# Mixer phase of a two-block transformer kernel: two heads across the partitions, block-diagonal 128x128 products, attention written between the levels of the triangular inverse

## The reference, cut to what matters

```python
z = rmsnorm(h, mix_norm_g) @ w_in                     # 256 x 3072
y_pool = pool_mixer(z[:, :256])                       # 4 windowed means, 4 small products, a scale
y_rwkv = rwkv7_mixer(z[:, 256:1280])                  # 4 heads of 64
y_diff = diff_attention(z[:, 1280:])                  # 4 heads, two score maps each
h = h + concat([y_pool, y_rwkv, y_diff]) @ w_out
# rwkv7_mixer: token shift, low-rank decay/a/gate, normalized key, the wkv7 recurrence, group norm, gate
# diff_attention: q, k RMS-normalized over 64 channels per (token, head, c);
#   p = softmax(s0 + bias) - lam * softmax(s1 + bias);  o = p @ v;  RMS norm of o over 128, gain
```

## Time and profile before

| | us |
|---|---|
| median of 3 runs | 3002.99 (2996.99 to 3004.98) |
| the profiled execution's own time | 3003.37 |
| its span | 3001.6 |
| mixer phase in it, first transpose to the last addition | 2177.7 to 2595.5 |

### The profile page before, as it was taken

One profiled execution on the slowest core, in us unless ns is written; L12 is line 12 of the kernel. 1 busy time (PEld: TensorE's weight loads), 2 busy tenths in 40 slices (PEclk: granted clock), 3 DMA queues, 4 the chain that ended last, 5 costly groups with the idle time before them and its releaser, 6 DMA issues.

```text
span 3001.6 us, 42198 instructions
## 1 busy us (share of the span) xinstructions
PE 2597.4 (87%) x16904; PEld 2319.8 (77%) x16904; DVE 2282.8 (76%) x3225; ACT 874.9 (29%) x1292; POOL 266.1 (9%) x100
## 2 busy tenths in 40 slices
PE   6979999999999996689999999999875674595898
PEld 6857999999888875379999998888673573474896
DVE  6768897999666777378989996666785645585887
ACT  1000344444555440103444445555312000000000
POOL 0000593000000000005920000000000000000000
PEclk8999999999999997689999999999996555697999
DMA  5624676656777763026765657777551000241554
GB/s 183 179 84 134 203 210 186 191 179 189 244 256 241 243 208 103 32 92 207 210 190 179 191 179 252 255 241 242 181 148 60 1 15 0 81 154 42 148 171 145
DMA packets 201186, 484.00 MB, mean 161 GB/s; under 512 B 23392, under 2 KB 93408, under 8 KB 200480
## 3 DMA queue, kind: packets, MB, share of 16 engines
q1 hardware_dynamic: 194784, 467.75, 50.1%
q10 hardware_dynamic: 6208, 13.56, 1.4%
HBM read 446.62 MB, written 34.60 MB: 160 GB/s over the span
## 4 chain that ended last, share of the span: by engine, by line
PE 58%; DVE 32%; POOL 4%; issue 2%; DMA 2%; ACT 1%; ACTq 0%; DVEq 0%
PE psum L865 23%; PE psum L662 19%; DVE rounded L1251 7%; DVE halves L2021 7%; PE psum L818 6%; DVE halves L2018 5%; POOL rounded L630 4%; PE psum L1040 2%; DVE rounded L1247 2%; DMA sb<-in_u_turned 1%; DVE sb L1764 1%; PE psum L704 1%; PE psum L943 1%; DVE sb L1286 1%; PE psum L941 1%
## 5 line engine op out<-in xcount | busy, mean ns | idle before, releaser
L1251 DVE TENSOR_TENSOR rounded<-sb,rounded 128x1024 fp32r<-128x1024 f32 (+3 forms) x696 | 813.9, 1172 | 243.0 <-ACT rounded L2242 233.4
L662 PE MATMUL psum<-rounded 128*128 128x256 f32 (+1 forms) x4380 | 728.8, 330 | 84.4 <-DVE rounded L1251 42.3
L818 PE MATMUL psum<-rounded 128*128 128x256 f32 x6144 | 774.2, 285 | 12.6 <-POOL rounded L630 12.4
L662 PEld LDWEIGHTS psum<-rounded 128*128 128x128 f32 x4380 | 655.6, 198 | 157.8 <-DVE rounded L1251 38.8
L2242 ACT ACTIVATE rounded<-sb 128x1024 fp32r<-128x1024 f32 x512 | 542.8, 1060 | 788.5 <-PE psum L818 346.6
L818 PEld LDWEIGHTS psum<-rounded 128*128 128x128 f32 x6144 | 748.1, 192 | 15.2 <-POOL rounded L630 15.2
L865 PE MATMUL psum<-rounded,weights 128*128 128x512 f32 x3072 | 697.3, 389 | 0.4 <-ACT sb L2258 0.4
L865 PEld LDWEIGHTS psum<-rounded,weights 128*128 128x128 f32 x3072 | 576.4, 188 | 120.6 <-issue 1.2
L630 POOL TENSOR_TENSOR rounded<-sb,rounded 128x1024 fp32r<-128x1024 f32 x96 | 265.9, 2785 | 1255.8 <-ACT rounded L2242 1255.3
L1247 DVE CAST rounded<-sb 128x1024 fp32r<-128x1024 f32 (+4 forms) x317 | 192.9, 609 | 134.5 <-PE psum L662 110.0
L2021 DVE TENSOR_TENSOR halves<-halves,small 128x1536 bf16<-128x1536 bf16 x128 | 225.0, 1758 | 4.4
(11 more groups left out here) (292 smaller groups left out, 1439.1 us busy)
## 6 DMA issues: line engine op xcount, KB each, us to landing
sb<-in_u_turned SPq DMA_DIRECT2D x256, 512.0 KB, 3.8
sb<-in_peer_v SPq DMA_DIRECT2D x256, 512.0 KB, 3.6
hidden<-sb SPq DMA_DIRECT2D x256, 128.0 KB, 3.8
sb<-hidden SPq DMA_DIRECT2D x256, 128.0 KB, 3.5
sb<-in_ret_w_in SPq DMA_DIRECT2D x48, 512.0 KB, 4.4
sb<-in_ffn_w_up SPq DMA_DIRECT2D x40, 512.0 KB, 4.5
sb<-in_peer_w_q SPq DMA_DIRECT2D x32, 512.0 KB, 4.1
sb<-in_ffn_w_down SPq DMA_DIRECT2D x22, 512.0 KB, 4.0
```

The source lines that it names most:

```text
L662: mm = pe.matmul(o, a[p], b[q], start=(first and i == 0), stop=(last and i == 2), skip_group_check=True)
L818: mm = pe.matmul(ps(bank, 1)[:, 0:T], u[p][:, k * P:(k + 1) * P], hT[:, q, k, :], start=(k == 0 and w == 0), stop=(k == KD - 1 and w == 2))
L1251: vec.tensor_tensor(ring_lo[0:k, part, 0:wide], ring[0:k, slot, 0:wide], ring_hi[0:k, part, 0:wide].bitcast(F32), ALU.subtract).then_inc(c ...
```

## The change

Only the mixer phase and what feeds it are rewritten.

- **Layout.** Two heads lie across the 128 partitions: channel tensors are 128x512 where they were 64x1024, and there are 8 pair units (`PU`) where there were 16 units. Where a product needs both heads apart, one operand is block-diagonal 128x128 (`btB`, `ktB`, `mabA`, `makA`, `makR`, `RB`, `AV`, `Tm`, `TmT`, `Q`, `Mt`), written by quadrants; the zeros are set by GpSimd at the start.
- **Norms.** The sums of squares of q and k are products with a 128x2 matrix (`each`), so 32 numbers a token; one root and one reciprocal on 128x32 (`qki`). k is scaled through a widened copy turned by TensorE (`wide`, "kb"); q's factor goes into the scores' scale. The o norm is a Square with a sum on ScalarE.
- **Weights.** ScalarE makes the high halves of the phase's 56 tiles (`BY_ACT`, `hi_to`), VectorE only the low ones.
- **Parameters** are issued by SP between the tiles of `slots0` from its fourth on, after a wait for the end of the peer phase; the bias by SP after the last tile of `pool_in`, after a wait for `ktB`.
- **Order.** Each engine has a list of named steps and one semaphore; the others wait for a step by name. The preparation lies between the panels; q.k scores, Exp, the pool mixer and the turning of p lie between the levels. Each level is done in two halves of 4 pair units. GpSimd makes `aoff` for levels 1 to 5; the copies of X go to ScalarE. Level 0 needs no product.
- **Softmax.** Four quarters (map, token block): the max as the bias of Exp, the sum from Exp's accumulator, the division folded into the difference.
- **`mix_out`** takes its rows in the order 0, 1, 4, 5, 6, 7, 2, 3 (`MIX_OUT_ROWS`), and begins when the pool part is there; the recurrence's part comes last.

The core of the diff (TensorE, levels and end):

```diff
+                for b in range(1, LEVELS):
+                    pe.wait_ge(*pool_told.of(f"aoff{b}"))
+                    for half, us in zip("AB", HALVES):
+                        pe.wait_ge(*vec_told.of(f"T{b - 1}{half}" if b > 1 else "T0"))
+                        tell(units(6, P, lambda u: a["aoff"][b % 2][:, u, :], of("Tm"), us), f"X{b}{half}")
+                    if b == 1:
+                        tell(turned(0, of("ktB")), "kT")
...
+                    if b == 2:
+                        pe.wait_ge(*act_told.of("aT"))
+                        scores(0)
...
+                    for half, us in zip("AB", HALVES):
+                        pe.wait_ge(*act_told.of(f"X{b}{half}"))
+                        if b < LEVELS - 1:
+                            tell(units(4, P, of("TmT"), of("X"), us), f"T{b}{half}")
+                        tell(units(2, P, of("X"), of("TmT"), us), f"W{b}{half}")
...
+                for half, us in zip("AB", HALVES):
+                    pe.wait_ge(*vec_told.of(f"T5{half}"))
+                    tell(units(4, P + C, of("TmT"), of("AV"), us), f"AV{half}")
+                turn_p(0)
...
+                tell(units(4, 2 * P, of("G1"), of("RB"), [u for u in range(PU) if u % NC_]), "QM")
+                tell(turn_p(1), "pT")
...
+                panel("mix_out", lambda k: hk(MIX_OUT_ROWS[k]), "tokens", 0, D, between=join)
```

VectorE between the levels, ScalarE's high halves and GpSimd:

```diff
+                    if b > 1:
+                        biased(b - 2)
+                    for half, us in zip("AB", HALVES):
+                        part = slice(us[0], us[-1] + 1)
+                        if b < LEVELS - 1:
+                            vec.wait_ge(*pe_told.of(f"T{b}{half}"))
+                            vec.tensor_tensor(a["Tm"][:, part, :], a["Tm"][:, part, :], banks_of(4, us), ALU.add)
+                        vec.wait_ge(*pe_told.of(f"W{b}{half}"))
+                        vec.tensor_tensor(a["TmT"][:, part, :], a["TmT"][:, part, :], banks_of(2, us), ALU.add)
+                    if b > 1:
+                        tops(b - 2)
+                    if b == 4:
+                        combine(0)
...
+            def hi_to(end_):
+                while ahead.n < end_:
+                    n = ahead.n
+                    k, wide = chunk_size[n]
+                    act.wait_ge(ring_loaded[n % RING], 16 * (n // RING + 1))
+                    act.wait_ge(chunks_done, n - SPLIT + 1)
+                    act.activation(ring_hi[0:k, n % SPLIT, 0:wide], ring[0:k, n % RING, 0:wide], ACT.Copy)
+                    ahead.up()
...
+                for b in range(1, LEVELS):
+                    if b > 2:
+                        gp.wait_ge(*pe_told.of(f"X{b - 2}B"))
+                    gp.tensor_tensor(a["aoff"][b % 2], a["mabA"], bcast(a["levels"][:, b, :], 1, PU), ALU.mult)
...
+            def mixer_params(count):
+                if len(mixers_left) == len(params["mixers"]):
+                    sync.wait_ge(phase_done, phases.index("mixers"))
+                for dst, src in mixers_left[:count]:
+                    sync.dma_start(dst, src).then_inc(params_loaded, 16)
```

More of the change, by code:

```diff
@@ L502, in build, with over @@
[L502 to L506 removed]
+                def over(at, *dims):
+                    return Memory(at, 0, at.shape[1]).take(*dims)
+                B2 = (PU, P)
+                hn = m.take(2048)
@@ L1035, in pe_mixers, with tell @@
-                pe.wait_ge(*masked)
-                wait_all(turned)
-                def units(b0, lhs, rhs, first=True, last=True, us=range(UN)):
-                    for u in us:
-                        mm = pe.matmul(ps(b0 + u // 8, 1, C)[:, (u % 8) * C:(u % 8 + 1) * C], lhs(u), rhs(u),
-                                       start=(first and u % 8 == 0), stop=last, skip_group_check=True)
+                told = Count()
+                def tell(mm, name):
+                    pe_told.check(name, told.up())
+                    mm.then_inc(mix_pe, 1)
@@ new lines, in units @@
+                def units(b0, wide, lhs, rhs, us=range(PU), begin_=True, last=True, parts_=P):
+                    per, begun = BANK // wide, set()
+                    for u in us:
+                        b = b0 + u // per
+                        mm = pe.matmul(ps(b, 1, parts_)[:, (u % per) * wide:(u % per + 1) * wide], lhs(u), rhs(u),
+                                       start=(begin_ and b not in begun), stop=last, skip_group_check=True)
+                        begun.add(b)
+                    return mm
@@ L1667, in vec_mixers @@
+                vec.memset(z[:, :, 0:1], 0.0).then_inc(*own.next())
+                split_to(end["slots0"] + 2)
                 vec.wait_ge(params_loaded, loads["mixers"])
                 done()
[L1669 to L1672 removed]
@@ new lines, in vec_mixers @@
+                split_to(end["slots1"] + 3)
+                vec.wait_ge(*act_told.of("z1"))
+                mixed(6, 8, "zm_act")
+                more(1, "pool_in")
+                mixed(4, 6, "zm")
+                more(1, "pool_in")
+                vec.wait_ge(*act_told.of("kkn"))
+                vec.tensor_scalar(a["kk2"], a["kk2"], 1e-12, None, ALU.max).then_inc(*own.next())
+                done()
+                more(1, "pool_in")
+                for hb in range(2):
+                    vec.reciprocal(a["kk2"][:, hb, :], a["kk2"][:, hb, :]).then_inc(*own.next())
+                    more(1, "pool_in")
@@ new lines, in vec_mixers @@
+                for w, dst in enumerate(quadrants(a["btB"])):
+                    half = slice(w * C, (w + 1) * C)
+                    vec.tensor_tensor(dst, u3(a["kk2"])[half], u3(a["Pi"])[half], ALU.mult).then_inc(*(tell("btB") if w else own.next()))
+                split_to(end["slots3"] + 3)
+                more(3, "pool_in")
+                split_to(end["diff_v"] + 1)
+                vec.wait_ge(*pe_told.of("qksum"))
+                for w, scale in enumerate((float(C), 1.0)):
+                    vec.tensor_scalar(a["qki"][:, w].rearrange("p b h c -> p (b h c)"), ps(1, 1)[:, w * 16:(w + 1) * 16],
+                                      scale / C, scale * RMS_EPS, ALU.mult, ALU.add).then_inc(*(tell("qkvar") if w else own.next()))
@@ new lines, in vec_mixers @@
+                more(1, "pool_in")
+                qki = a["qki"].rearrange("p w b h c -> p (w b h c)")
+                vec.wait_ge(*act_told.of("qkn"))
+                vec.reciprocal(qki, qki).then_inc(*tell("qkinv"))
+                for w, dst in enumerate(quadrants(a["ktB"])):
+                    half = slice(w * C, (w + 1) * C)
+                    vec.tensor_tensor(dst, u3(a["kx"])[half], u3(a["Pi"])[half], ALU.mult).then_inc(*(tell("ktB") if w else own.next()))
+                more(1, "pool_in")
@@ new lines, in vec_mixers, with banks_of @@
+                more(2, "pool_in")
+                done()
+                unit = bcast(ident, 1, PU)
+                vec.tensor_tensor(a["TmT"], unit, a["aoff0"], ALU.add).then_inc(*own.next())
+                more(2, "pool_in")
+                vec.wait_ge(*act_told.of("mabA"))
+                masked(quadrants(a["RB"][:, :, 0:P]), 4, 1, lambda i: a["before"][:, 1, :], "mabR")
+                split_to(end["pool_in"])
+                def banks_of(b0, us=range(PU)):
+                    return ps(b0, 2).rearrange("p (u t) -> p u t", t=P)[:, us[0]:us[-1] + 1, :]
@@ new lines, in act_mixers, with levels, exps @@
+                hi_to(end["pool_in"] + 3)
+                def levels(b):
+                    for half, us in zip("AB", HALVES):
+                        from_pe(f"X{b}{half}")
+                        act.activation(a["X"][:, us[0]:us[-1] + 1, :], ps(6 + us[0] // 4, 1).rearrange("p (u t) -> p u t", t=P),
+                                       ACT.Copy).then_inc(*tell(f"X{b}{half}"))
+                def exps(q):
+                    c, tb = q % 2, q // 2
+                    from_vec_(f"mx{q}")
+                    for hd in range(4):
+                        v = a["p"][:, c, tb, hd, :]
+                        act.activation(v, v, ACT.Exp, bias=a["top"][:, q, hd:hd + 1], accum_out=a["sum"][:, q, hd:hd + 1]).then_inc(
+                            *(tell(f"ex{q}") if hd == 3 else own.next()))
```

1079 lines of the change are left out of this document (611 added, 468 removed), and 5 rows, old and new, of the table PE_TOLD.

## The result

The changed kernel takes 2818.39 us (median of four runs, 2812.15 to 2820.47), the kernel before 3002.59: ratio 0.939, interval 0.9365 to 0.9406, so 184 us or 6% faster. 2802 was predicted, with a range of 2768 to 2862. Timed again later, the same kernel had a median of 2813.5 (2805.1 to 2823.9), ratio 0.9388 [0.9357, 0.9419].

A forecast was written before the change was run, and what follows sets the result against it. The mixer phase was taken as bound by a serial chain between PE and DVE, not an engine. Terms 95 + 50 + 37 + 26 and 10 of hand-overs gave 218 us against 419, so 2802 us, range 2768 to 2862.

The forecast's parts named there:

- Projections, preparation and the way to X: Start of the mixer phase to the first X: 95 us, against 167 before.
- Levels: The mixer phase's five levels: 50 us against 111 before, from 41 of PE products, 3 of delay, 5 of late halves.
- Recurrence, attention's end, norms: Stretch between the levels and `mix_out`: 37 us against 115 before, between 31 at full and 50 at half clock.
- `mix_out`: Last stretch of the mixer phase: 26 us, as before, with PE's matmuls at 24.
- signs: Mixer phase: `pool_in` ends at 90 us, a level 8 to 11, PEclk above 0.8 in levels, `mix_out` starts at 180.
- The clock: Mixer phase: mostly full clock in the levels, whose new products have 128 rows, and a mixed one behind them.
- Half clock through the levels: Rival: half clock in levels and recurrence, levels 86 us, recurrence 50, phase 272, kernel 2856; chance 22%.
- The projections' convoy: Rival: in-order engines and a ring of three hold the projections, 125 + 5 us instead of 95, kernel 2837; chance 14%.
- Better than forecast: Rival: mixer phase 183 us, from projections 85, levels 42, rest 31 and `mix_out` 25; kernel 2767; chance 12%.
- Nothing overlaps: Rival: named steps in the mixer phase overlap nothing; only norms (41), reciprocal and compact passes (15) and casts saved; 2943; chance 4%.
- GpSimd's masks: Rival: X of each level waits for `aoff`; slower than 3003 if the five masks take 43 us each, against 2.8; chance 3%.
- GpSimd beside DVE: Mixer phase: GpSimd's masks and gate products could add 0 to 18 us to DVE; taken as 0.

The follow-up runs named there:

- e5: The changed kernel, unedited, timed once more beside the later runs: 2813.5 us, ratio 0.9388 to the kernel before.
- e2: The changed kernel with ScalarE copying `pl` before it makes `mix_out`'s high halves: 2807.9 us, ratio 0.9351.
- e1: The changed kernel with the pool's 1 MB matrix loaded in eight pieces, one beside each tile of `slots1`: 2803.9 us, ratio 0.9351.
- e3: The changed kernel with GpSimd's zero fillings held until VectorE has made `kk2`: 2808.8 us, ratio 0.9360.
- e4: The changed kernel with the edits of e1, e2 and e3 together: 2800.5 us, ratio 0.9329.
- e9: e4 plus ten products with overwritten result while PE waits for the second combination, ahead of the recurrence: 2795.5 us, ratio 0.9311.
- e11: The kernel before, with the normalisation of q and k left out: 2976.3 us, ratio 0.9916.
- e6: The changed kernel with scores, bias, maximum and Exp behind the fifth level instead of between the levels: 2822.1 us, ratio 0.9410.
- e7: The changed kernel with the level products X, T and W contracting over partitions 0 to 63 only: 2822.0 us, ratio 0.9415.
- e12: e10 with each 128x128x128 level product made as two of 64x64x64, one a head, in opposite quarters of the array: 2792.0 us, ratio 0.9306.
- e8: The changed kernel with VectorE instead of ScalarE making the high halves of the phase's 56 tiles: 2811.8 us, ratio 0.9366.
- e10: e9 plus twenty more such products while PE waits for the attention's norm, before `mix_out`: 2788.7 us, ratio 0.9289.

## Why the prediction was right, and where it was not

*The bound of the phase, and the sum.* The prediction took the phase for a chain and summed 218 us. It measured 224.0 in the first profiled execution and 217.2 in e5. The terms:

- Projections, preparation and the way to X: 95, with 10 of hand-overs for the whole phase. Measured 111.0 (99.7 + 11.3) and 104.3 (95.4 + 8.9). This is the term that was mis-sized. Its working missed four things. ScalarE is put in front of the tiles' arrival, and so waits for DMA before work that others need (11.3 instead of 5.2, e2). The parameters on SP were given 2 to 5 us "while PE still waits for `hT`"; the large one came behind that point, 1.4 to 2.6 us of PE's waits (e1 against the two executions). The fillings of GpSimd had no price: 2.7 us (e3), ahead of the phase's first block. And the PE work was priced at full clock, where the 100 us of the projections had 0.93. With the three waits mended it is 99.9 us (e4: 94.7 + 5.2), the 95 and half of the hand-overs.
- Levels: 50, measured 47.9, in every execution whose levels are unchanged but e9 (49.2). The working by PE's products held in kind (41, measured 44.8 of busy time). The 3 us by which VectorE was to delay level 5 and the 5 for late halves came as two waits, 3.3 us together. That the total is right to 2 us is luck: one term is too small, the others too large.
- Recurrence, attention's end, norms: 37 between 31 at full and 50 at half clock, measured 38.6. e9 shows the full-clock value, 30.6.
- `mix_out`: 26, measured 26.5.

The phase thus saved 193.8 instead of 201 us. With 2.7 us from the fillings, 2.8 that the profiled execution was late before the phase, and 1.4 behind it, that makes up the 14 us by which the profiled execution missed the forecast. No run is about the 2.8 and the 1.4; the begin of the phase differs by several us between executions.

Of its signs, a level of 8 to 11 us (10.6) and PEclk above 0.8 in the levels (1.00) came out. The end of `pool_in` came 99.7 us after the start, not 90, and `mix_out` 197.5 us into the phase, not 180.

How the saving divides between layout, order and clock is shown only in part. The trace shows where the time went, stretch by stretch; e11 prices the norms in the old order at 26.6 us, e6 the place of the scores at 5. No run puts the preparation back behind the panels, or the old one-quarter products into the new order.

*The clock.* The forecast, "mostly full clock in the levels and a mixed one behind them", came out: 1.00 and 0.74. The reason given for it did not. The prediction read the earlier trace rows as "64-row products keep the clock at 0.50". Products over 64 rows ran at 1.00 (e7), and so did 64x64x64 products in two quarters of the array (e12). So in the new order neither 128 rows nor 128x128 products are needed for it.

What the runs do show is falls behind idle time of PE: 2.33 us ahead of the recurrence (e4), 4.18 behind level 1 (e8), 4.13 before AV (e12), 1.82 three times (e6). Given work there, the clock stayed in e9 and e10. But the idle time does not settle it alone. It stayed at 1.00 behind 2.43 us in e6, and behind some 2 us before level 2 in eight executions (X at 2.26 us), while it fell behind the same 1.98 us in e9, and behind 0.88 in e12. One stretch speaks against the order as the only cause: in the earlier trace rows PE was busy for 27.56 of 28 us at 0.50, with 64x64 products that all used one quarter, and e11 repeats it (256 records in 27.57 us). That the levels' full clock comes from their gapless order is thus likely and not shown; that the old products in one quarter would have had it too is not known.

*Half clock through the levels* (first rival): no. The rule behind it, that transposes do not count as activity (the Trainium skill, "TensorE: Matmul & The Clock Gate", Part 4), would have had level 1's 16 turned blocks pull the clock down; the stretch of 2294 to 2342 shows 1.00. They stood in two groups of 8 between products, so the rule itself is not contradicted.

*The projections' convoy* (second rival) happened in part, 9 to 16 us over the 95, where the rival had 35. *Better than forecast*: its 31 behind the levels and its 25 for `mix_out` are those of e10 (29.8 and 24.6), but not of this kernel; its 42 for the levels came in no run that has the scores between them. *Nothing overlaps*: no; PE was busy for 44.82 of the levels' 48 us. The price of the norms inside this rival, 41, was wrong: 26.6 (e11), because most of the reciprocal lay beside PE in three of the four levels. *GpSimd's masks*: 2.34 to 2.35 us each, and PE waits for none of them; what they hold on VectorE comes next.

*GpSimd beside DVE* was taken as 0. It cost 2.7 us by the fillings, which write only, and the masks have a price too, which no run removes. In the changed kernel a pass of VectorE over 128x1 takes 2.04 us beside the third mask and ends with it; in e7, where it comes before the mask, it takes 0.15 (and the three roundings behind it 5.64 instead of 3.49). The roundings and the adds of level 1 queue behind it, and PE waits 2.07 us for the adds. From these rows I estimate 1.9 us for the mask. The roundings are of `mix_out`'s tiles, which PE needs some 80 us later; no run puts them behind the adds.

```profile
2296.27 2.35 POOL L742 TENSOR_TENSOR hT_bits<-sb 128x1024 f32<-128x1024 f32 x1 [2.69 <-PE psum L1100]
2296.60 2.04 DVE L1934 TENSOR_TENSOR sb<-sb 128x1 f32<-128x1 f32 x1
...
2298.75 3.49 DVE L1401 TENSOR_TENSOR rounded<-sb,rounded 128x1024 fp32r<-128x1024 f32 x3
...
2303.57 2.26 PE L1100 MATMUL psum<-sb,hT_bits 128*128 128x128 f32 x16 [2.07 <-DVE sb L1981]
```
 The Trainium skill ("SBUF — State Buffer", Who interferes with whom) names two cases: an instruction of VectorE with two SBUF inputs beside a GpSimd instruction that reads SBUF, and one in a two-port mode; the prediction weighed the first alone, and only for the levels' adds. The 128x1 pass has two SBUF inputs and is the first case. The pass that the fillings held (3.48 instead of 0.75 us) has one SBUF input and passes 1024 columns in 0.75 us, faster than the 1.22 of the earlier trace rows, so I take it for the second case; that it is in such a mode no view shows.

## What to carry to other kernels

When work is interleaved to fill a chain, look next at the last idle time of PE before a run of small products: with 2.3 us filled there by ten products thrown away, the stretch behind it was 8.6 us shorter (5.0 in the medians). It is a thing to try and measure, since idle times of the same length did not always lower the clock. An engine that is in order and takes over part of another's work must not be given what waits for a DMA ahead of a copy that the critical path needs; the same holds for roundings ahead of the adds. Read for each such line what is queued behind it. And before the price of a long instruction is put on the path, lay it beside the other engines' rows of the same microseconds.

## What the runs showed of the hardware

- Two 64x64x64 products in opposite quarters of the array overlap: 32 records of 64 columns took 1.15 us at a clock of 1.00, 36 ns each, against 115 at 0.50 in one quarter (e11, 32 in 3.67). By halving that I estimate 57 at full clock in one quarter; no row has it. The Trainium skill ("TensorEngine Tiling (Array Packing)", Key Properties) says that tiles work independently, and the trace agrees. The two-head layout is thus not the cheapest form for PE: X in 1.15 instead of 2.05 us. It brought only 1.8 us in the levels here, since the adds of VectorE were then waited for and the clock fell behind the waits.
- A fill by GpSimd, which reads nothing, held a pass of VectorE with a single input for 2.7 us (3.48 against 0.75, e3). A mask by GpSimd held a 128x1 pass with two SBUF inputs: 2.04 us against 0.15.
- Once down, the clock stayed near 0.50 through 20 us in which PE was busy for 19.99 (e4), and through 28 us of the kernel before. In a run of 128x128x128 products it came back; what makes the difference is open.
- The granted clock of the same code differs between executions: MK took 3.52 us in one execution of the changed kernel and 2.02 in the other, with 4.26 and 3.50 us of idle time before it.
